# Split weights: products of 256 columns in one PSUM half, tile by tile

## What is computed

```python
def first_block(x, ...):
    h = rms_norm(x, norm1_w)
    proj = h @ w_in                                     # q, kv, gates, DeltaNet q/k/v/z, merge gates
    o_nsa, o_dn = nsa_mixer(...), gated_deltanet(...)   # sparse attention; chunked recurrence
    g_nsa, g_dn = split(sigmoid(merge_g))
    x = x + (g_nsa * (o_nsa @ w_up_nsa) + g_dn * (o_dn @ w_up_dn)) @ w_o
    h2 = rms_norm(x, norm2_w)
    return x + (silu(h2 @ w_ffn_gate) * (h2 @ w_ffn_up)) @ w_ffn_down

def second_block(x, ...):
    proj = rms_norm(x, attn_norm_g) @ w_in_2            # RWKV-7 inputs, loras, latents
    x = x + concat(rwkv7_mixer(...), mla_mixer(...)) @ w_out_2
    h = rms_norm(x, ffn_norm_g)
    return x + (silu(conv3(h @ w_gate_2)) * (h @ w_up_2)) @ w_down_2
# reference = rms_norm(second_block(rms_norm(first_block(x), norm_f_w)), final_norm_g_2)
```

## Time and profile before

| | us |
|---|---|
| median of 3 runs | 2822.27 (2820.22 to 2822.90) |
| the profiled execution | 2820.33 |
| its span, first to last instruction | 2818.5 |
| TensorE busy | 2771.2 (98%) |
| TensorE weight loads busy | 2434.1 (86%) |
| VectorE busy | 2023.7 (72%) |
| ScalarE busy | 1364.0 (48%) |
| GpSimd busy | 479.3 (17%) |
| HBM read over the span | 469.8 MB, 167 GB/s |

### The profile page before, as it was taken

How to read it: one execution, slowest core, us unless ns; L and a number is a source line. 1 busy time by engine, 2 the same in 40 slices (tenths; PEclk the granted TensorE clock), 3 DMA queues, 4 the chain that set the end, 5 groups by cost and what they waited for, 6 DMA issues and landing times.

```text
span 2818.5 us, 42260 instructions
## 1 busy us (share of the span) xinstructions
PE 2771.2 (98%) x16660; PEld 2434.1 (86%) x16660; DVE 2023.7 (72%) x3102; ACT 1364.0 (48%) x2051; POOL 479.3 (17%) x526
## 2 busy tenths in 40 slices
PE   8999999999999999999999999999999999999998
PEld 7888888888888888888888888878998888888887
DVE  7987797776776666656657888878677777667655
ACT  6453455455555445434435545434454444444434
POOL 2211011110111111001102635421111111001101
PEclk9999999999999999999999999999999999999999
DMA  6444333455555555555556534221365555555555
GB/s 227 162 160 159 121 116 132 145 191 188 193 187 190 192 191 191 192 190 193 188 183 199 177 124 133 92 76 53 120 202 191 191 192 189 193 188 194 189 180 164
DMA packets 133396, 474.65 MB, mean 168 GB/s; under 512 B 14800, under 2 KB 15056, under 8 KB 132944
## 3 DMA queue, kind: packets, MB, share of 16 engines
q1 hardware_dynamic: 133200, 471.96, 50.3%
HBM read 469.80 MB, written 2.10 MB: 167 GB/s over the span
## 4 chain that ended last, share of the span: by engine, by line
PE 90%; DVE 5%; ACT 2%; POOL 1%; issue 1%; DMA 0%; SPq 0%; DVEq 0%; ACTq 0%; POOLq 0%
PE ps L899 90%; DVE U L1869 1%; DVE ringl L1869 1%; POOL U L2551 1%; ACT high L1409 1%; PE ps L902 1%; POOL U L2624 0%; ACT U L1409 0%; DVE U L1878 0%; DVE xT L1869 0%; DMA xT<-in_x_dram 0%; DVE hx L1869 0%; DVE U L2067 0%; ACT hr L1409 0%; DVE U L1875 0%
## 5 line engine op out<-in xcount | busy, mean ns | idle before, releaser
L899 PE MATMUL ps<-hr,high 128*128 128x512 f32 x4672 | 1491.4, 397 | 11.8 <-DVE ringl L1869 10.8
L1869 DVE TENSOR_TENSOR ringl<-ring,high 128x1024 fp32r<-128x1024 f32 x888 | 1082.6, 1221 | 435.1 <-ACT high L1409 434.6
L1409 ACT ACTIVATE high<-ring 128x1024 fp32r<-128x1024 f32 x888 | 915.6, 1033 | 601.6 <-PE ps L899 590.7
L899 PEld LDWEIGHTS ps<-hr,ringl 128*128 128x128 f32 x4672 | 879.2, 188 | 192.5 <-issue 1.4
L899 PE MATMUL ps<-hr,ringl 128*128 128x256 f32 x4672 | 924.3, 279 | 0.0
L899 PEld LDWEIGHTS ps<-hr,high 128*128 128x128 f32 x4672 | 717.6, 188 | 21.0 <-issue 15.1
L899 PE MATMUL ps<-yur,high 128*128 128x512 f32 (+1 forms) x2432 | 682.9, 370 | 3.8 <-DVE xT L1869 2.2
L2551 POOL TENSOR_TENSOR U<-U,rs 128x256 f32<-128x256 f32 x292 | 264.5, 906 | 1688.3 <-DVE U L1869 1668.8
L899 PEld LDWEIGHTS ps<-yur,ringl 128*128 128x128 f32 x2176 | 400.0, 188 | 79.6
L1409 ACT ACTIVATE U<-ps 128x256 f32<-128x256 f32 (+3 forms) x481 | 172.8, 371 | 592.0 <-PE ps L899 567.6
L899 PE MATMUL ps<-yur,ringl 128*128 128x256 f32 x2176 | 429.9, 279 | 0.0
(11 more groups left out here) (178 smaller groups left out, 1250.2 us busy)
## 6 DMA issues: line engine op xcount, KB each, us to landing
ring<-in_w_dram SPq DMA_DIRECT2D x862, 512.0 KB, 3.3
ring<-in_w_dram SPq DMA_DIRECT2D x48, 256.0 KB, 3.3
xT<-in_x_dram SPq DMA_DIRECT2D x3, 512.0 KB, 8.1
out_dram<-hx SPq DMA_DIRECT2D x3, 512.0 KB, 2.7
cst<-in_cst_dram SPq DMA_DIRECT2D x1, 1374.5 KB, 12.5
yT<-in_lora_dram SPq DMA_DIRECT2D x1, 1024.0 KB, 7.4
xT<-in_x_dram SPq DMA_DIRECT2D x2, 256.0 KB, 4.5
U<-in_lora_dram SPq DMA_DIRECT2D x1, 512.0 KB, 5.4
```

The source lines that it names most:

```text
L899: return e.matmul(out, l, r, start=start, stop=stop)
L1409: return e.activation(out, i, ACT.Copy, scale=scale)
L1869: return e.tensor_tensor(out, a, b, op)
```

## The change

Every unit of split weights now has all its products in the left half of the bank. For each tile TensorE issues three products of 256 columns: high weights with low(x), high weights with high(x), low weights with high(x). `halves` and `both` are gone, and so is the special path for `wout`. Since only one half is filled, ScalarE's copy alone frees the bank of the units that it copies (`half` and `rest` are gone), GpSimd waits for that copy, and `down` and `wo` need one add, not two. In the planner the cost of a tile and the lists of steps follow.

```diff
-TILE, TILE4, TILE33, ROWS = 0.348, 0.432, 0.23, 0.72
+TILE, TILE4, TILE33, ROWS = 0.342, 0.432, 0.23, 0.69
...
             own = [u for u in ends if not sums_x(u)]
-            both_ = [u for u in ends if not one_half(u)]
+            scaled_ = [u for u in ends if normed(u)]
+            added = [u for u in ends if sums_x(u)]
+            merged = [u for u in ends if u.kind == "up"]
...
-            work["DVE"].append((m - 0.5, sum(0.42 if u.kind == "wout" else 0.85 if sums_x(u) else 0.9 if u.kind == "up" else 0.43 for u in both_) + 0.4 * later.count("up"),
-                                [("end" if sums_x(u) else "half", u.i) for u in both_], [("free", u.i) for u in both_]))
-            work["POOL"].append((m - 0.5, 1.1 * len(both_), [("free", u.i) for u in both_], [("data", u.i) for u in both_]))
+            work["DVE"].append((m - 0.5, 0.42 * len(added) + sum(0.9 if u.key[0] else 0.48 for u in merged) + 0.4 * later.count("up"),
+                                [("end", u.i) for u in added] + [("free", u.i) for u in merged], [("free", u.i) for u in added]))
+            work["POOL"].append((m - 0.5, 1.1 * len(scaled_), [("free", u.i) for u in scaled_], [("data", u.i) for u in scaled_]))
...
-                            c = mact if one_half(prev) else mdve
+                            c = mdve if sums_x(prev) else mact
                             e.wait_ge(c.sem, c.after("free", prev.i))
...
-                                if u.kind == "wout":
-                                    for n_, half in enumerate(moving(u, k0 + k)):
-                                        mm(out[:, 0:SEQ], wh, half, start and n_ == 0, False)
-                                else:
-                                    mm(shaped(out[:, :], 2, SEQ), wh, halves(u, k0 + k), start, False)
-
-                                for j in (k, k - 1) if k % 2 else ():
-                                    w = slice(at + j * nc_, at + j * nc_ + 128)
-                                    t = mm(out[:, 0:SEQ], ringl[:, w], moving(u, k0 + j)[0], False, stop and j == k - 1)
+                                xh, xl = moving(u, k0 + k)
+                                mm(out[:, 0:SEQ], wh, xl, start, False)
+                                mm(out[:, 0:SEQ], wh, xh, False, False)
+                                t = mm(out[:, 0:SEQ], ringl[:, w], xh, False, stop)
...
-                copy(place_of(u), src).then_inc(mact.sem, mact.inc("free" if one_half(u) else "half", u.i))
+                copy(place_of(u), src).then_inc(mact.sem, mact.inc("free", u.i))
...
-            def rest(u, dst):
-
-                e.wait_ge(mact.sem, mact.after("half", u.i))
-                tt(dst, dst, ps[u.bank][:, SEQ:2 * SEQ], ADD).then_inc(mdve.sem, mdve.inc("free", u.i))
-
             def evac0(u):
...
                 if u.kind == "up":
                     part, t = key
                     s = sg[t % 4]
-                    rest(u, um[:, t % 2, :])
                     e.wait_ge(mact.sem, mact.after("sig", 16 * part + t))
-                    e.wait_ge(mdve.sem, mdve.last())
+                    e.wait_ge(mact.sem, mact.after("free", u.i))
...
-                elif u.kind in ("wo", "down", "wout"):
-                    x = xT[:, key[-1], :]
+                elif sums_x(u):
+                    x, src = xT[:, key[-1], :], ps[u.bank][:, 0:SEQ]
...
-                    parts = 1 if u.kind == "wout" else 2
-                    for j in range(parts):
-                        src = ps[u.bank][:, SEQ * j:SEQ * j + SEQ]
-                        if u.kind == "wo":
-                            i = stt(x, src, 0.5, x, MUL, ADD)
-                        else:
-                            i = tt(x, x, src, ADD)
...
+                    i = stt(x, src, 0.5, x, MUL, ADD) if u.kind == "wo" else tt(x, x, src, ADD)
+                    i.then_inc(mdve.sem, mdve.inc("free", u.i))
...
                 if normed(u):
-                    e.wait_ge(mdve.sem, mdve.after("free", u.i))
+                    e.wait_ge(mact.sem, mact.after("free", u.i))
```

More of the change, by code:

```diff
@@ L766, in build, with normed @@
             needs[units[index[("rw", q, 0)]].first()] = [(f"rw{q % STREAMS}", (q // STREAMS - 2) * len(RECUR) + taken)]
[L768 to L770 removed]
         def sums_x(u):
             return u.kind in ("wo", "down", "wout")
+        def normed(u):
+            return u.kind in ("gates", "dn", "q", "kc", "vc", "ks", "kw", "mg", "gate", "fup", "lora", "rw", "lat")
         work = {"PE": [], "ACT": [], "DVE": [], "POOL": []}
@@ L877, in place_of @@
             return (flat if u.kind == "uq" else kn)[:, key[0], :]
-        def normed(u):
-            return u.kind in ("gates", "dn", "q", "kc", "vc", "ks", "kw", "mg", "gate", "fup", "lora", "rw", "lat")
         rs_read = {"norm2": index[("mg", 1, 15)], "attn_g": index[("fup", 1, 43)], "ffn_g": index[("rw", 7, 2)],
                    "final_g": index[("fup", 2, 43)]}
-        def both(a, b):
-            a, b = min(a, b) - y_at, max(a, b) - y_at
-            x = min(a, b - a - SEQ)
-            return yur[:, a - x:2 * b - a - x].rearrange("p (t n) -> p t n", t=2)[:, :, x:x + SEQ]
         block = ctx.enter_context(nc.Block())
@@ L917, in sums @@
                 i.then_inc(mpe.sem, mpe.inc("sum", tag))
-            def halves(u, k):
-                if u.kind in ("up", "wout"):
-                    t = 8 * u.key[0] + k if u.kind == "up" else OUT[u.key[0]][k]
-                    return both(y_high[u.kind == "wout"][t], y_at + SEQ * t)
-                if u.kind == "wo":
-                    return both(mixh_at + SEQ * k, u_at + mark1 + SEQ * k)
-                if u.kind == "down":
-                    return axr[:, 16 * (u.key[1] % 2) + k, :, :]
-                return hxr[:, k, :, :]
             def moving(u, k):
@@ L1963, in evac1 @@
                     e.wait_ge(mpool.sem, mpool.after("sc", u.i))
+                    e.wait_ge(mdve.sem, mdve.after("tb", f, t))
                     stt(alF[:, at, :], tb[:, t % 4, :], 0.5, ub[:, t % 4, :], MUL, MUL).then_inc(mdve.sem, mdve.inc("v", f, t))
```

12 lines of the change are left out of this document (1 added, 11 removed).

## The result

The changed kernel takes 2875.19 us (2873.39 to 2878.74, 4 runs), the kernel before 2821.24 us (2819.47 to 2822.90, 4 runs) beside it: 1.0193 of the time, 95% interval 1.0175 to 1.0211, or 54 us more. The forecast was 34 us less, with a chance of 0.03 for slower. In square brackets behind a ratio stands its 95% interval. The span of the profiled execution is 2876.9 us, against 2818.5.

A forecast was written before the change was run, and what follows sets the result against it. TensorE was taken as the bound, busy 2771.2 of 2818.5 us. Gains of 31.7 us (6336 tiles) and 2.6 us (256 up tiles), waits unchanged, took 2820.3 to 2786.0 profiled, 2788.0 as median; range 2775 to 2802.

The forecast's parts named there:

- GpSimd's earlier start: In units that ScalarE copies, GpSimd's scaling starts behind that copy, 0.4 us earlier; on no path, costed at nothing.

The follow-up runs named there:

- e7: Kernel before with each 512-column product split into two of 256, one per bank half, evacuations and planner costs as before; 2860.45 us, 1.0132 of before.
- e6: Changed kernel with each tile's low-weight product issued as two of 128 columns, so four products and four full loads a tile; 3548.48 us.
- e12: Changed kernel with the low product as two of 128 columns, each loading 64 weight columns, low weights of the upper 64 output channels left out; 3233.78 us.

## What to carry to other kernels

A pace read from a short stretch is one sample: look for the same form elsewhere in the trace and in a second execution before a sum of thousands of tiles goes by it. Keep one long product instead of two short ones where a bank has room, even if that costs an engine with slack 180 us. When a change also alters a planner's costs, time the new costs with the old products and the old costs with the new ones, since where side steps stand can put TensorE at half clock and one of the two runs alone can mislead. Tune the costs by stage.

## What the runs showed of the hardware

- A stream of fp32r products of 256 columns, each with its own load of 128 columns, runs at 113.3 or 117.8 ns a product, at a granted clock of 1.00. Which one can differ between executions of one program (w_out in the two traces of the kernel before). The up units of e7 take 350 ns for three.
- 512 columns in one product take 228 to 230 ns. A full load takes 113 ns at least (e6: 453 ns for four products and four loads); 128 columns with a load of 64 take 60, and the wait for a full load behind them is recorded one product later (e12).
- VectorE's operations on two inputs of 256 elements take 0.42 us, and more where GpSimd has just begun a multiplication. In the two groups above, 129 operations of the changed kernel begin while GpSimd works, and take 0.74 us (the 84 subtractions) and 0.76 us (45 others) on the mean, 0.98 at most; the 187 that meet none take 0.42. Before, 127 overlap a multiplication with VectorE first and take 0.42; only 4 begin behind it. Timelines of VectorE and GpSimd in the changed kernel:

```profile
2605.79 0.77 DVE L1853 SCALAR_TENSOR_TENSOR U<-U 128x256 f32<-128x256 f32 x1 [0.97 <-ACT U L1520]
```

```profile
2605.52 0.74 POOL L2509 TENSOR_TENSOR U<-U,rs 128x256 f32<-128x256 f32 x1 [5.01 <-ACT U L1384]
```

Before, VectorE's operation came first (2602.76) and GpSimd's, begun at 2602.93, took 0.86. GpSimd's earlier start, costed at nothing, brought them together the other way round. This agrees with the Trainium skill (SBUF — State Buffer, section "Who interferes with whom"), by which an operation of VectorE with two inputs from SBUF and one of GpSimd that reads SBUF contend; the durations by who came first bear it out here, though no run took one of the two away.
